# Branch sums and the MLP's squares worked in PSUM banks, with banks, table loads, high parts and heads in another order

## The reference

```python
# first block
h = rms_norm(x, attn_norm); q, k, v = split(h @ w_in)
mixed = [moba_attention(...), diff_attention(...)]   # 8 + 4 heads, the latter with two maps each
x = x + mixed @ w_out
x = x + peer_ffn(rms_norm(x, ffn_norm), ...)         # 128 expert rows gathered per token
# second block
proj = rmsnorm(x, norm_mix_g) @ w_in_2
branches = [conv_out, stick_breaking, retention]     # three, of width 512
up = einsum('bsnw,nwd->bsnd', branches, w_branch)
merged = sum_n sigmoid(gate_logits[n] + b_gate[n]) * up[n]
x = x + merged @ w_o
x = x + softmax(q_h k_h^T) v_h @ w_xo                # 4 heads of 256 over 256 memory rows
x = x + square(relu(rmsnorm(x, norm_mlp_g) @ w_up)) @ w_down
return rmsnorm(x, final_g)
```

## Time and profile before

| | |
|---|---|
| median of 3 runs | 1397.77 us (1397.28 to 1398.6) |
| profiled execution | 1396.3 us |
| its span | 1394.5 us |
| PE busy | 1244.4 us, 89% |
| POOL busy | 894.8 us, 64% |
| DVE busy | 800.9 us, 57% |
| ACT busy | 612.0 us, 44% |
| DMA, mean over the span | 287 GB/s; 423 to 427 in the row stage |
| chain that ended last | PE 55%, DMA 22%, DVE 9%, POOL 6%, ACT 4% |

### The profile page before, as it was taken

The page is one execution under the profiler, slowest core; times in us unless marked ns, Lnnn a source line. Parts: engine busy times, 40 slices in busy tenths (PEclk is TensorE's granted clock), DMA queues, the critical chain, the costliest instruction groups (busy, mean ns, idle before and its releaser), DMA issues.

```text
span 1394.5 us, 17408 instructions
## 1 busy us (share of the span) xinstructions
PE 1244.4 (89%) x5974; PEld 888.7 (64%) x5974; DVE 800.9 (57%) x1575; ACT 612.0 (44%) x1296; POOL 894.8 (64%) x533
## 2 busy tenths in 40 slices
PE   7999999888888987777887898999999899999997
PEld 6878874444444532332333344799999888899886
DVE  6934398768777667777667744603643722266301
ACT  5566534343443442332323333447464345555432
POOL 5734766556766646554544441996868864799985
PEclk9999999999999999899999999999999999999999
DMA  7632589999999999999999996474546633466662
GB/s 266 192 103 78 169 331 387 427 426 425 427 425 425 425 427 426 427 426 427 427 427 423 424 427 258 151 212 136 182 123 219 202 107 121 136 184 193 200 198 102
DMA packets 72944, 400.64 MB, mean 287 GB/s; under 512 B 8096, under 2 KB 8352, under 8 KB 39712
## 3 DMA queue, kind: packets, MB, share of 16 engines
q0 software_dynamic: 36864, 268.45, 45.9%
q1 hardware_dynamic: 33696, 123.35, 27.3%
q10 hardware_dynamic: 2304, 7.79, 1.5%
HBM read 396.42 MB, written 3.15 MB: 287 GB/s over the span
## 4 chain that ended last, share of the span: by engine, by line
PE 55%; DMA 22%; DVE 9%; POOL 6%; ACT 4%; issue 4%; ACTq 0%; SPq 0%; POOLq 0%; DVEq 0%
DMA arena<-in_experts,arena 21%; PE bank L602 13%; PE bank L603 13%; PE bank L604 13%; PE bank L898 10%; DVE arena L1773 4%; POOL w_lo L1415 3%; POOL arena L1459 2%; PE bank L655 1%; PE bank L664 1%; ACT arena L1226 1%; ACT diag L1232 1%; PE bank L1023 1%; ACT w_hi L1052 1%; ACT arena L1065 1%
## 5 line engine op out<-in xcount | busy, mean ns | idle before, releaser
L1415 POOL TENSOR_TENSOR w_lo<-ring,w_hi 128x1024 fp32r<-128x1024 f32 x222 | 565.9, 2572 | 180.1 <-ACT w_hi L1052 179.6
L898 PE MATMUL bank<-arena,diag 128*128 128x512 f32 x968 | 457.7, 625 | 93.3 <-ACT diag L1232 93.3
L1459 POOL DMA_INDIRECT arena<-in_experts,arena x242 | 289.2, 1195 | 240.5 <-PE bank L898 167.1
L1773 DVE CUSTOM_DVE_ANT_0 arena<-arena 128x1024 f32<-128x1024 f32 x242 | 322.0, 1343 | 166.4 <-DMA arena<-in_experts,arena 165.1
L898 PEld LDWEIGHTS bank<-arena,diag 128*128 128x128 f32 x968 | 186.9, 199 | 344.3 <-issue 210.3
L1052 ACT ACTIVATE w_hi<-ring 128x1024 fp32r<-128x1024 f32 x228 | 239.9, 1058 | 164.1 <-PE bank L604 130.0
L602 PE MATMUL bank<-hT_hi,w_hi 128*128 128x256 f32 x736 | 210.9, 287 | 4.5 <-DVE hT_lo L1494 2.7
L604 PE MATMUL bank<-hT_hi,w_lo 128*128 128x256 f32 x736 | 207.4, 282 | 0.0
L603 PE MATMUL bank<-hT_lo,w_hi 128*128 128x256 f32 x736 | 207.3, 282 | 0.0
L1223 ACT ACTIVATE arena<-arena 128x2 f32<-128x2 f32 (+2 forms) x99 | 20.2, 204 | 410.0 <-DVE arena L1773 409.9
L602 PEld LDWEIGHTS bank<-hT_hi,w_hi 128*128 128x128 f32 x736 | 140.3, 191 | 10.1 <-issue 8.8
(11 more groups left out here) (251 smaller groups left out, 1661.0 us busy)
## 6 DMA issues: line engine op xcount, KB each, us to landing
ring<-in_stream SPq DMA_DIRECT2D x228, 512.0 KB, 3.6
arena<-in_experts,arena POOLq DMA_INDIRECT x242
kv_park<-arena ACTq DMA_DIRECT2D x8, 256.0 KB
arena<-kv_park ACTq DMA_DIRECT2D x1, 2048.0 KB, 7.7
x_res<-in_x SPq DMA_DIRECT2D x2, 512.0 KB, 5.0
arena<-in_mem SPq DMA_DIRECT2D x1, 1024.0 KB, 10.9
arena<-in_sub_keys ACTq DMA_DIRECT2D x1, 1024.0 KB, 5.6
out<-arena SPq DMA_DIRECT2D x2, 512.0 KB, 2.6
```

Of the source, the lines that this page charges most:

```text
L898: mm = pe.matmul(y_banks[half][:, :], diag[:, slot % DIAGS, :], rows_buf[BUFFER[slot]][:, D + 512 * half:D + 512 * half + 512], start=(i = ...
L1415: nc.gpsimd.tensor_tensor(w_part(w_lo_mem, c), ring[:, c % RING, :], w_part(w_hi_mem, c).bitcast(F32), ALU.subtract).then_inc(S("lo_made"), 1)
L1459: nc.gpsimd.indirect_dma_start(out=rows_buf[b], out_offset=None, in_=experts, in_offset=bass.IndirectOffsetOnAxis(ap=expert_u[:, slot:slot ...
L1773: v.tensor_tensor_reduce(out=rows_buf[b][:, 0:D], in0=xn[:, slot // (PEER_H * PEER_K), :], in1=rows_buf[b][:, 0:D], scale=1.0, scalar=0.0, ...
```

## The change

1. **Banks.** `plan` moves on by two after the last group of the memory's transposes; every bank of a later result outside the row stage's own stages is another one.
2. **Start.** ACT makes only what a group needs ahead of it (`ahead` 0 for 1), with chunk 1's high part ahead of the third group. PE runs six filling matmuls in the first bank of w_in (`keep_busy`).
3. **Attention.** At step 3 the memory's pieces go ahead of the score, waiting for the norm's groups one by one. ACT copies the last heads at step 3 of its loop, not 4.
4. **Exp and Ln.** Both Exps, then both Lns, with one chunk's high part between each two.
5. **Branch sums** of n = 1 and 2 are worked in the bank; for n = 2 ACT copies the high part out of it, and the cast goes. w_o waits for the evacuation of those banks.
6. **High parts** of the last chunk go ahead of the first square sum for xa and mlp too.
7. **Cross attention.** PE waits for each xq copy by itself, and runs six filling matmuls ahead of the first xpT, behind its bank's wait and ahead of that for the probabilities.
8. **MLP.** DVE makes max(x, 0) times Relu's output in the bank and subtracts the low part from it; it now evacuates the bank. Relu and Square on ACT are joined by a semaphore. POOL's norm of mlp comes behind the low parts up to mlp_down's eighth chunk in its program, tile by tile.

```diff
@@ plan
-                turn = bank + 1
+                turn = bank + (2 if key == ("mem", "hT", 3) else 1)
@@ natural (PE)
                 out_t = [open_bank(pe, (name, n, t)) for t in range(TT)]
+                if name == "w_in" and n == 0:
+                    keep_busy(out_t[0], 6)
@@ attention (PE)
                 if step == 5:
                     turn_heads(TURN_ORDER[6:])
-                if step < 12:
-                    for m in maps_of(HEAD_ORDER[step]):
-                        score(m, 4 if step == 0 and m == MAP_ORDER[0] else 0)
+                for m in maps_of(HEAD_ORDER[step]) if step < 12 and step != 3 else ():
+                    score(m, 4 if step == 0 and m == MAP_ORDER[0] else 0)
...
-                    if keys_done(step) == 0:
-                        for g in range(4):
-                            normed("mem")(g)
                     for piece in range(keys_done(step), keys_done(step + 1)):
+                        if piece < KT and piece % 2 == 0:
+                            normed("mem")(piece // 2)
                         memory(piece)
+                for m in maps_of(HEAD_ORDER[step]) if step == 3 else ():
+                    score(m)
@@ w_o and cross attention (PE)
-                natural("w_o", ... pe.wait_ge(S("merged"), g + 1) ...)
+                natural("w_o", ... wait_evacuated(pe, ("branch", 2, g // 2, g % 2)) ...)
...
-            for c in range(4):
-                wait_evacuated(pe, ("xq", c))
             pe.wait_ge(S("kv_loaded"), 16)
             for h in range(4):
+                wait_evacuated(pe, ("xq", h))
                 bank = open_bank(pe, ("xs", h))
...
-                    pe.wait_ge(S("xprobs"), step + 1)
-                    turn(("xpT", step), [...])
+                    turn(("xpT", step), [...],
+                         6 if step == 0 else 0, (S("xprobs"), step + 1))
@@ hi_before, sumsq, norm_out (ACT)
-                ahead = last + RING - 1 if last >= 0 else 1
+                ahead = last + RING - 1 if last >= 0 else 0
...
-                    hi_parts(... last - 1 if n == 0 and name != "mix" else last if t == 0 else last + RING - 1)
+                    hi_parts(... last - 1 if n == 0 and name in ("ffn", "final") else last if t == 0 else last + RING - 1)
...
+                    if name == "attn" and g == 2:
+                        hi_parts(1)
@@ attention, exp and ln (ACT)
-                if step == 4:
+                if step == 3:
                     heads_out(TURN_ORDER[6:])
...
             for q in range(2):
-                hi_parts(LAST["in_sqk"] + RING + 2 * q)
+                hi_parts(LAST["in_sqk"] + RING + q)
                 act.wait_ge(S("abs_ready"), q + 1)
                 e = ebuf[:, 4 * q:4 * q + 4, :]
-                own.link(nc.scalar.activation(e, e, ACT.Exp))
+                own.mark(nc.scalar.activation(e, e, ACT.Exp))
+            for q in range(2):
+                hi_parts(LAST["in_sqk"] + RING + 2 + q)
+                own.sync()
+                e = ebuf[:, 4 * q:4 * q + 4, :]
                 nc.scalar.activation(e, e, ACT.Ln, bias=1.0).then_inc(S("log_ready"), 1)
@@ branch high parts (ACT)
+            for i in range(4):
+                key = ("branch", 2, i // 2, i % 2)
+                hi_before(key)
+                act.wait_ge(S("summed"), i + 1)
+                nc.scalar.activation(hT_hi[:, 2 * i:2 * i + 2, :], <bank of key>, ACT.Copy)\
+                  .then_inc(S("merged_hi"), 1)
@@ mlp (ACT)
-                    act.wait_ge(S("hidden"), c - 3)
+                    wait_evacuated(act, ("mlp_up", c - 4))
...
-                own.link(nc.scalar.activation(relu[c % 4], bank[:, :], ACT.Relu))
+                nc.scalar.activation(relu[c % 4], bank[:, :], ACT.Relu).then_inc(S("relu"), 1)
+                act.wait_ge(S("relu"), c + 1)
@@ norms (POOL)
-            for name in ("xa", "mlp", "final"):
-                norm(name)
+            norm("xa")
+            lo_parts(FIRST["mlp_down"] + 7)
+            for t in range(TT):
+                norm_tile("mlp", t)
+            norm("final")
@@ branch sums (DVE)
+            def merged_low(i):
+                key = ("branch", 2, i // 2, i % 2)
+                dve.wait_ge(S("merged_hi"), i + 1)
+                v.tensor_tensor(hT_lo[:, 2 * i:2 * i + 2, :], <bank of key>,
+                                hT_hi[:, 2 * i:2 * i + 2, :].bitcast(F32), ALU.subtract).then_inc(evac_sem(key), 1)
...
-                            v.tensor_tensor(g2, <bank>, g2, ALU.mult).then_inc(evac_sem(key), 1)
-                            wait_evacuated(dve, key)
-                            own.mark(v.tensor_tensor(merge[:, k:k + 2, :], merge[:, k:k + 2, :], g2, ALU.add))
-                        if n == 2:
-                            own.sync()
-                            own.link(v.tensor_copy(hT_hi[:, k:k + 2, :], merge[:, k:k + 2, :]))
-                            v.tensor_tensor(hT_lo[:, k:k + 2, :], merge[:, k:k + 2, :],
-                                            hT_hi[:, k:k + 2, :].bitcast(F32), ALU.subtract).then_inc(S("merged"), 1)
+                            own.link(v.tensor_tensor(gated, gated, g2, ALU.mult))
+                            if n == 1:
+                                v.tensor_tensor(merge[:, k:k + 2, :], gated, merge[:, k:k + 2, :], ALU.add)\
+                                 .then_inc(evac_sem(key), 1)
+                            else:
+                                v.tensor_tensor(gated, gated, merge[:, k:k + 2, :], ALU.add).then_inc(S("summed"), 1)
+                                if k:
+                                    merged_low(k // 2 - 1)
+            merged_low(KT // 2 - 1)
@@ mlp (DVE)
-                wait_evacuated(dve, ("mlp_up", c))
-                r, sq = relu[c % 4], square[c % 4]
-                own.link(v.tensor_tensor(sq, r, r, ALU.mult))
+                dve.wait_ge(S("relu"), c + 1)
+                own.link(v.scalar_tensor_tensor(bank[:, :], bank[:, :], 0.0, relu[c % 4], ALU.max, ALU.mult))
+                dve.wait_ge(S("hidden_hi"), c + 1)
                 <low part: bank in place of sq, then evac_sem in place of "hidden">
```

More of the change, by code:

```diff
@@ L493, in build @@
         relu = [A(2048 + 512 * i, 512) for i in range(4)]
-        square = [A(4096 + 512 * i, 512) for i in range(4)]
         y_out = tiles(A(6144, 2048))
@@ L995, in _ @@
             for n in range(2):
-                natural("w_o", 4, n, h_, FIRST["w_o"], (lambda g: pe.wait_ge(S("merged"), g + 1)) if n == 0 else None)
+                natural("w_o", 4, n, h_, FIRST["w_o"], (lambda g: wait_evacuated(pe, ("branch", 2, g // 2, g % 2))) if n == 0 else None)
             norm("xa", xs)
@@ L1013, in _ @@
                 if step < 4:
-                    pe.wait_ge(S("xprobs"), step + 1)
-                    turn(("xpT", step), [xp[:, step, t, m * P:(m + 1) * P] for m in range(2) for t in range(TT)])
+                    turn(("xpT", step), [xp[:, step, t, m * P:(m + 1) * P] for m in range(2) for t in range(TT)],
+                         6 if step == 0 else 0, (S("xprobs"), step + 1))
                 if step == 0:
@@ L1035, in _ @@
                 natural("mlp_down", 16, n, lambda k: (hid_hl[:, 0, k, :], hid_hl[:, 1, k, :]), FIRST["mlp_down"],
-                        (lambda i: pe.wait_ge(S("hidden"), i + 1)) if n == 0 else None)
+                        (lambda i: wait_evacuated(pe, ("mlp_up", i))) if n == 0 else None)
         @block.scalar
@@ L1090, in sumsq @@
                         continue
-                    hi_parts(last + 2 if name == "ffn" and n and not t else last - 1 if n == 0 and name != "mix" else last if t == 0 else last + RING - 1)
+                    hi_parts(last + 2 if name == "ffn" and n and not t else last - 1 if n == 0 and name in ("ffn", "final") else last if t == 0 else last + RING - 1)
                     for key, tile, cols in nat_keys(ADDED[name]):
@@ L1972, in _ @@
             for c in range(16):
[L1973 to L1977 removed]
+                bank = banks[at["mlp_up", c][0][0]]
+                dve.wait_ge(S("relu"), c + 1)
+                own.link(v.scalar_tensor_tensor(bank[:, :], bank[:, :], 0.0, relu[c % 4], ALU.max, ALU.mult))
+                dve.wait_ge(S("hidden_hi"), c + 1)
+                v.tensor_tensor(hid_hl[:, 1, 2 * c:2 * c + 2, :], bank[:, :].rearrange("p (j t) -> p j t", j=2),
+                                hid_hl[:, 0, 2 * c:2 * c + 2, :].bitcast(F32), ALU.subtract)\
+                 .then_inc(evac_sem(("mlp_up", c)), 1)
             dve.wait_ge(S("rstd"), 2 * seq["mlp"] + TT)
```

11 lines of the change are left out of this document (6 added, 5 removed).

## The result

| | before | after |
|---|---|---|
| median | 1398.11 us (1397.28 to 1398.6, 4 runs) | 1375.05 us (1373.39 to 1376.12, 4 runs) |
| profiled execution, span | 1394.5 us | 1371.6 us |
| PE busy | 1244.4 us | 1230.7 us |
| DVE busy | 800.9 us | 762.9 us |
| POOL busy | 894.8 us | 873.7 us |

The ratio is 0.9842, with a 95% interval of 0.9831 to 0.9854. The forecast was 1376.7 us in 1368.5 to 1387.

A forecast was written before the change was run, and what follows sets the result against it. Outside the DMA-paced row stage, PE's stops, half-clock stretches behind them and matmul pace were taken as the bound. Terms 0 - 7.0 - 1.7 - 7.3 - 2.0 - 2.7 - 0.4 = -21.1 us gave 1376.7 us, range 1368.5 to 1387.

The forecast's parts named there:

- Start: w_in: six filling matmuls and ACT's reordered high weights were taken to change nothing, 0 us (range -1.6 to +1.4).
- Attention: Attention steps 2 and 3: stops of 1.46 and 1.34 us and half of two slow stretches go, -7.0 us (-2 to -8).
- Exp and Ln: Ahead of in_conv's product: an earlier copy removes PE's 1.58 us stop and slow first matmul, -1.7 us (0 to -1.9).
- Branch sums: w_o: in-bank sums at 0.68 us remove PE's 4.61 us stop and half the slow stretch, -7.3 us (-3 to -7.4).
- Square sums: xa and mlp: earlier last high parts remove two PE stops, -1.0 us each, -2.0 together (-0.5 to -2.2).
- Cross attention: Waits per head ahead of xs -1.0, fillings in the wait ahead of xpT -1.7: -2.7 us (-0.7 to -2.8).
- MLP: mlp_up: PE's short wait at 1219.7 goes, -0.4 us; the slower pace of 172 matmuls in 20 us stays.
- rival (a): mlp_up keeps the pace of 177 matmuls in 20 us, 2.2 us less: 1374.5 us; chance 0.25.
- (b): Attention keeps its low clock, -2 to -4.5 us instead of -7: about 1380.5 us; chance 0.15.
- (c): An operation into a bank costs 2.48 us, not 0.68; branches give 3, mlp nothing: about 1381.4 us; chance 0.08.
- (d): mlp_up: DVE's in-bank pair and POOL's subtracts shut each other out, 27 us more: 1404 us; chance 0.03.

The follow-up runs named there:

- e2: Changed kernel with attention all as before (banks on by one, step 3's score first, last heads at ACT's step 4): 1380.43 us, ratio 0.988.
- e5: Changed kernel with the bank shift behind the memory's group 3 alone undone, attention's new orders kept: 1376.46 us, ratio 0.9863.
- e8: Changed kernel with Exp and Ln in the old order and the last chunk's high part behind the first square sum: 1380.71 us, ratio 0.9896.
- e1: Changed kernel with branch sums as before: products and sums in SBUF, cast and low part by DVE: 1377.05 us, ratio 0.9857.
- e7: Changed kernel without the six filling matmuls at w_in and the six ahead of the first xpT: 1373.19 us, ratio 0.9842.
- e12: Changed kernel without both fillings and with PE waiting for all four xq copies ahead of xs: 1372.49 us, ratio 0.9832.
- e9: Changed kernel run once more, nothing altered: 1372.12 us, ratio 0.9827.
- e4: Changed kernel with POOL's norm of the MLP in its old place, squares still in the bank: 1373.99 us, ratio 0.9832.
- e11: Changed kernel with ACT's last heads copied at step 4 as before, step 3's order and the bank shift kept: 1374.32 us, ratio 0.9845.

## Why the prediction was right, and where it wasn't

- **Start, 0.** w_in ended at 79.10 for 79.14. By luck: the filling's price was mis-sized by half, since six fillings are twelve rows and not six, and where they ran at half speed, in part or in whole, w_in ended 1.5 to 3.1 us later. The means of the ten profiles with it and the four without differ by 1.2 us.
- **Attention, -7.0.** Measured -7.4 (-7.5 by e2), and step 7's score at 104.1 for 104.5. The sum held, one reason didn't: that the low clock comes from the stop of 1.46 us falls with e5. With the orders new, the shift that removes the stop is worth 0.9 us; with the shift kept, the orders are worth 6.15. The first stop isn't gone in full either, 0.61 us of it are left.
- **Exp and Ln, -1.7.** Measured -1.8 (e8).
- **Branch sums, -7.3.** w_o to xq fell by 8.1, of which 0.8 is the square sum's (e8): -7.3. e1 shows the cause, DVE's operations without a PSUM operand beside POOL, and the PSUM output priced by the PSUM input (0.68 to 0.70) was right. The reason given, that each operation now has one SBUF operand, is too wide: the cast had one input there too and was slow. e1 puts back sums, cast and wait together, so what ACT's copy in place of the cast gives by itself wasn't measured. e1 gave 5.8, as its slow stretch was 3.4 us and not 6.7: the stop of 4.5 us came back both times, the clock's share was 1.3 and 2.7.
- **Square sums, -2.0.** Measured -1.9.
- **Cross attention, -2.7.** Measured -2.3, near by luck. The step that failed is the -1.7 for the wait ahead of xpT: the fillings stand in the wait for the probabilities and don't shorten it. Without them it is still 1.80 us (e7), with them PE is busy for 2.75, which takes 0.6 us more. What came in its place is the clock: e12, with both stops and no filling, is 1.6 us shorter than the kernel before, about half of the slow stretch of 3.3, for which the sum had nothing here. The wait per head gives 1.25 (e12 against e7). The slow stretch is gone in all, with the filling or not. What brought the clock down there is open.
- **MLP, -0.4, or 2.2 more if the fast pace holds.** Measured -3.5: rival (a) came true in the first profile. Of the changed kernel and the twelve runs, seven profiles have mlp_up at 90.7 us and six at 87.4; the program of the first profile and of e9 is the same, and it is once here and once there. So most of the 3.5 is chance. The kernel before ran its first four chunks at the fast pace and fell to the slow one at its pause for POOL, as rival (a) had it:

```profile
1220.17 0.35 PE L602 MATMUL bank<-hT_hi,w_hi 128*128 128x256 f32 x1 [0.23 <-POOL w_lo L1415]
```

That pause isn't needed for the slow pace: the seven profiles at 90.7 us have none in mlp_up. Whether it can bring it wasn't tested, since e4 didn't bring the pause back. An estimate of the edit's own share is 0.5 us: the 90.84 before, plus 0.4 for its 96 fast matmuls (0.0044 us each), less 90.70.
- The branches' +1.25 is the same chance the other way. With mlp_up's 3.0 (3.5 less 0.5) and this taken out, the profiled gain is 22.9 - 3.0 + 1.25 = 21.2, against a forecast of 21.1. That they agree so closely is chance too, as the start and cross attention show.
- Rivals (b), (c) and (d) fell: no slow stretch in attention, 0.70 us per in-bank operation, POOL with 9 us of slack in mlp_up between 1195 and 1270 us.

## What to carry to other kernels

A chain of small operations on VectorE with all operands in SBUF took three to six times as long beside GpSimd's long subtracts as alone (2.19, 2.48 and 2.71 us for 0.69, 0.43 and 0.69); leaving the value in its PSUM bank, so that each has a PSUM operand, took that away at no cost that the traces show. Filling matmuls didn't shorten the wait they stood in; all that they could have saved here is the clock behind it. Each stop cost about its own length or more (1.58 us ahead of in_conv's product cost 1.8, 1.34 in e11 cost 2.3), and a slow clock came behind it only sometimes: look at what the engine does next, and price a filling by its rows in the trace before putting it into a wait. Where a profile shows the same stage at two speeds, profile the same kernel twice before giving an edit the credit.
